# Who copies the first three tiles of the third branch's projection out of PSUM: VectorE instead of ScalarE

## The chip, the cores and the metric

One NeuronCore of one Trainium2 chip runs the whole program. The metric is the device time of one execution in microseconds (us), as the median of several runs.

## The reference, cut to what matters

One decoder layer on 512 tokens of width 1024, in float32. Four mixers run beside each other on one projection of the normalised input, each is projected back to 1024 channels, weighted by a sigmoid gate, and summed:

```python
z = h @ w_in                       # columns: aq ak av iq ik iw pin gu gv sq sk sv, then four gates
o_a = sparse_indexed_attention(...)   # 4 heads of 64, each query keeps its top 128 keys
o_b = multiscale_pool(...)
o_c = chunked_spatial_gating(...)
o_d = stick_breaking_attention(...)
o = jnp.stack([o_a, o_b, o_c, o_d], axis=2)
proj = jnp.einsum('bsnw,nwd->bsnd', o, w_branch)         # 256 -> 1024 for each branch
merged = jnp.sum(sigmoid(gl) * proj, axis=2)
x = x + merged @ w_out
x = x + swiglu_ffn(rms_norm(x), ...)
```

The sparse attention of a block of 128 queries is: logits for 4 heads, plus a bias that masks the keys not chosen, a row maximum, exp, division by the row sum, and the product with the values.

## The kernel before, in words

**Weights in chunks.** All weights come in chunks of 1 MB, numbered c. SyncE loads chunk c into one of two raw buffers (L395) once VectorE has finished the low half of chunk c-2. Each chunk is split into two reduced-precision parts: ScalarE writes the high part `w_hi` (L541, or in two halves at L549), then VectorE subtracts and writes the low part `w_lo` (L977). TensorE multiplies with three matmuls for each product (`three`, L1539: lines 1541, 1542, 1543) and can start a chunk only when both parts are there (semaphores `hi_ready`, `lo_ready`, L1846 and L1847).

**Order of the chunks around the change.** Chunk 15 is the projection of the first branch (m=0), 16 that of m=1, 17 to 20 are the gates of m=1, 21 is the projection of the third branch (m=2), 22 to 25 are its gates, 26 is the projection of m=3 and 27 to 30 are its gates. `PROJ_AT` is [15, 16, 21, 26]. "Chunk 21" below is the projection that the change touches.

**A projection chunk** (`proj_chunk`, L1572) makes 8 tiles d=0 to 7, each of 128 output channels by 512 tokens, from 6 matmuls. Tile f goes to PSUM bank f%2, so TensorE has two banks to fill in turn and waits in `take_bank` (L1545) until the tile two before has been copied out (semaphores `taken0`, `taken1`). For chunks 16, 21 and 26 ScalarE copies each tile to `branch` in SBUF (`branch_tiles`, L618, copy at L630). Into these copies it puts the two halves of the high part of the next chunk's weights: before tile 1 and before tile 4. VectorE does the low part of that chunk when the second half is there. For chunk 15 VectorE itself empties the banks (L1331), multiplying with the gates on the way.

**Gates.** For chunks 17 to 20 and 22 to 25 ScalarE writes the sigmoid of each tile from PSUM to `two` (L685), VectorE multiplies it with the tile of `branch` (`gated`, L1279), and GpSimd adds the result to `merged` (L521).

**The sparse attention lies between the chunks**, one block b of queries at a time, by `slot(c)` on each engine, which runs behind the engine's own work on chunk c. `A_SLOT` is 16. Block 2 goes: in slot 20 TensorE computes the values of block 1 (L1773) and the logits of block 2 (L1755, L1757), then goes on with chunk 21. VectorE adds the bias and takes the maxima (`biased`, L1198), ScalarE then negates them and takes the exponentials (`soft_max`, L748 and L750), and VectorE takes the reciprocal of the sums and multiplies (`normalised`, L1205 and L1207). In slot 21, behind chunk 21, TensorE transposes the result (L1764) and ScalarE copies it out (L759).

**Order on each engine.** Every engine works its instructions in the order of the code and stops at a wait. ScalarE's order here is: sigmoids of chunk 20, `soft_max(2)`, `branch_tiles(21)` with the halves of chunk 22, `turned_prob(2)`, the high part of chunk 23, sigmoids of chunk 22. VectorE's is: low part of chunk 21, products of chunk 20, `biased(2)`, `normalised(2)`, low part of chunk 22, five rounds of the search for the largest 8 scores of block 3 (`top_rounds(21)`, L1081 and L1082), low part of chunk 23, products of chunk 22, `biased(3)`.

Of the kernel before, what the change touches and what calls it, by code (L numbers as in the profile page):

```python
# [42 lines left out]
def hybrid_layer(nc, x, mix_norm, w_in, attn_q_norm, attn_k_norm, pool_w, pool_scale, gmlp_norm,  # L43
# [4 lines left out]
    TT = SEQ // P  # L48
    KT = D // P
# [18 lines left out]
    chunks = []  # L68
# [28 lines left out]
    PROJ_AT = [c for c in range(MIXER_CHUNKS) if chunks[c][0] == "proj"]  # L97
# [23 lines left out]
    fill_at, f = [], 0  # L121
# [10 lines left out]
    def w_at(c):  # L132
        if c < MIXER_CHUNKS:
            return c % 2 * CHUNK
        if chunks[c][0] == "ffn":
            return (7 * QUAD, 0)[(c - MIXER_CHUNKS) % 2]
        at = PLAIN[0] if c in PLAIN else max(d for d in down_at if d <= c)
        return (8 * QUAD, 0)[(c - at) % 2]
# [4 lines left out]
    def before_at(c):  # L143

        a, z = w_at(c), w_at(c) + w_size(c)
        return max((d for d in range(c) if w_at(d) < z and a < w_at(d) + w_size(d)), default=None)

    with ExitStack() as ctx:
        top = [(nc.sbuf_base + 63) // 64 * 64]

        def place(name, shape, dt=F32, at=None):
            size = 4
            for n in shape[1:]:
                size *= n
            if at is None:
                at = top[0]
                top[0] += (size + 63) // 64 * 64
            return nc.alloc_sbuf_tensor_at(name, shape, dt, offset=at)

        def sem(name):  # L160
            return ctx.enter_context(nc.semaphore(name))
# [23 lines left out]
        branch = place("branch", [P, KT, SEQ], at=L0)  # L185
# [107 lines left out]
        bank = [ctx.enter_context(nc.psum_tensor(f"bank{i}", [P, 512], F32)) for i in range(8)]  # L293
# [40 lines left out]
        S = {n: sem(n) for n in names}  # L334
        taken = [S["taken0"], S["taken1"]]
        raw_ready = [S["raw0"], S["raw1"]]
        x_ready = [S["x0"], S["x1s"], S["x2"], S["x3"]]
        hi_ready, lo_ready, filled = S["hi_ready"], S["lo_ready"], S["filled"]
# [15 lines left out]
        def head_rows(h):  # L354

            return (slice(0, 64), slice(64, 128))[::1 if h % 2 == 0 else -1]
        D_SLOT, A_SLOT = 10, 16
        IDX_SLOT = 2

        def split_early(c):  # L360

            return IDX_SLOT <= c - 2 < IDX_SLOT + 4

        def wait_taken(eng, f):

            eng.wait_ge(taken[f % 2], f // 2 + 1)
# [5 lines left out]
        def wait_used(eng, c):  # L372

            kind, _, _, _, what = chunks[c]
            if kind == "ffn":
                eng.wait_ge(S["product_done"], 7 * (wino_index[c] + 1))
            elif kind != "acc":
                eng.wait_ge(filled, fill_at[c + 1])
            elif what[3]:
                eng.wait_ge(S["acc_filled"], TT * (what[0] + 1))  # L380
            else:
                eng.wait_ge(S["acc_chunks"], sum(k[0] == "acc" and not k[4][3] for k in chunks[:c + 1]))
# [143 lines left out]
        def _(act):  # L526
# [16 lines left out]
            def split_half(c, second):  # L543
                n = chunks[c][2] * chunks[c][3] // 2
                part = slice(n * second, n * (second + 1))
                if not second:
                    act.wait_ge(raw_ready[c % 2], 16 * (c // 2 + 1))
                    wait_used(act, before_at(c))
                ins = nact.activation(w_hi[:, w_at(c) + part.start:w_at(c) + part.stop], raw[:, c % 2, part], ACT.Copy)  # L549
                if second:  # L550
                    ins.then_inc(hi_ready, 1)
# [66 lines left out]
            def branch_tiles(c):  # L618

                m = chunks[c][4]  # L620
                for d in range(KT):
                    if d in (1, 4):
                        split_half(c + 1, d == 4)
                    f = fill_at[c] + d
                    if m == 1:
                        wait_taken(act, fill_at[c - 1] + d)
                    else:
                        act.wait_ge(S["gated"], (m - 2) * KT + d + 1)
                    act.wait_ge(filled, f + 1)
                    nact.activation(branch[:, d, :], bank[f % 2][:, :], ACT.Copy).then_inc(taken[f % 2], 1)  # L630
# [61 lines left out]
            def indexer(b):  # L692

                for h in range(IDX_HEADS):
                    n = IDX_HEADS * (b - 1) + h
                    act.wait_ge(S["idx_filled"], n + 1)
                    if n >= 4:
                        act.wait_ge(S["relu_used"], n - 3)
                    w = P * (b + 1)
                    nact.activation(relu[:, n % 4, 0:w], bank[2 + n % 4][:, 0:w], ACT.Relu).then_inc(S["relu_ready"], 1)  # L700
# [68 lines left out]
            def slot(c):  # L769
                if IDX_SLOT <= c < IDX_SLOT + 3:  # L770
                    indexer(c - IDX_SLOT + 1)
                if c == 1:
# [190 lines left out]
        def _(dve):  # L963
            vec = nc.vector
            steps = [0]

            def link(ins):
                steps[0] += 1
                ins.then_inc(S["dve_step"], 1)
                dve.wait_ge(S["dve_step"], steps[0])  # L970
# [9 lines left out]
            def split_half(c, second):  # L980
                n = chunks[c][2] * chunks[c][3] // 2
                part = slice(n * second, n * (second + 1))
                at = slice(w_at(c) + part.start, w_at(c) + part.stop)
                dve.wait_ge(hi_ready, c + 1)
                ins = vec.tensor_tensor(w_lo[:, at], raw[:, c % 2, part], w_hi[:, at].bitcast(F32), ALU.subtract)
                ins.then_inc(lo_ready if second else S["dve_step"], 1)
                steps[0] += not second
# [199 lines left out]
            def biased(b):  # L1187
# [8 lines left out]
                for h in range(HEADS):  # L1196
# [2 lines left out]
                                             scalar=TAKEN, op0=ALU.add, op1=ALU.max,  # L1199
                                             accum_out=top_logit[:, h:h + 1]).then_inc(S["biased_ready"], 1)  # L1200

            def normalised(b):
                w = P * (b + 1)
                dve.wait_ge(S["prob_summed"], HEADS * (b + 1))
                link(vec.reciprocal(inv_total[:, :], total[:, :]))  # L1205
                for h in range(HEADS):
                    vec.tensor_scalar(prob[:, h, 0:w], prob[:, h, 0:w], inv_total[:, h:h + 1], None, ALU.mult)\  # L1207
                        .then_inc(S["prob_ready"], 1)
# [7 lines left out]
            def top_rounds(c):  # L1216
                for b, n in rounds.get(c, ()):
                    take_top(b, n, last=(c == max(d for d in rounds for e, _ in rounds[d] if e == b)))

            def slot(c):  # L1220
                if c == 1:
                    constants()
                if IDX_SLOT <= c < IDX_SLOT + 3:
                    if c == IDX_SLOT:
                        dve.wait_ge(S["iw_ready"], 1)
                        dve.wait_ge(S["const_made"], 4)
                    indexer(c - IDX_SLOT + 1)
                if c == 4:
                    wait_chunk_taken(dve, 3)
                    norm_sums()  # L1230
                if c == 5:
                    norm_scale()
                if c == 7:
                    gate_mixed()
                if c == 9:
                    out_parts(1, 6, PSC)
                if D_SLOT <= c < D_SLOT + HEADS + 2:
                    k = c - D_SLOT
                    if k >= 2:
                        stick_total(k - 2)  # L1240
                    if 1 <= k <= HEADS:
                        weights_low(k - 1)
                    if k < HEADS:
                        left(k)
                    if 2 <= k < HEADS:
                        stick_out(k - 2)
                    if k == HEADS + 1:
                        stick_out(HEADS - 2)
                        stick_out(HEADS - 1)
                        dve.wait_ge(S["q_hi_ready"], MT + 1)  # L1250
                        stack_low(True, qT, lambda x: slice(x, HEADS, 2), lambda own, x: q_lo[own, x:HEADS:2, :], 1.0)
                        dve.wait_ge(S["k_hi_ready"], MT + 1)
                        stack_low(False, kT, lambda x: slice(x, HEADS, 2), None, 1.0).then_inc(S["stacks_ready"], 1)
                if A_SLOT <= c <= A_SLOT + 2 * TT:
                    b, odd = (c - A_SLOT) // 2, (c - A_SLOT) % 2
                    if not odd and b < TT:
                        biased(b)
                        top_rounds(c)
                        normalised(b)
                    elif not odd:  # L1260
                        out_parts(3, 6, None)
# [23 lines left out]
            for c in range(MIXER_CHUNKS):  # L1285
# [37 lines left out]
                if (kind, what) == ("proj", 0):  # L1323
                    for d in range(KT):
                        if d in (2, 5):
                            split_half(c + 1, d == 5)
                        f = fill_at[c] + d
# [680 lines left out]
```

## Time and profile before

| | us |
|---|---|
| median of 3 runs | 799.18 (798.92 to 799.45) |
| the profiled execution, its own time | 797.43 |
| its span in the trace | 795.7 |
| TensorE busy in the span | 785.4 |
| VectorE busy | 516.8 |
| ScalarE busy | 369.6 |
| GpSimd busy | 89.4 |

Times in the trace are microseconds from the start of the span. PE is TensorE's matmul, PEld its weight load, which overlaps the matmuls, DVE is VectorE, ACT is ScalarE, POOL is GpSimd, SP is SyncE. Matmuls overlap in the records: one of 512 columns has a duration of 0.39 us, while the next one starts 0.23 us after it. A busy time of 99% is therefore no statement on how well the engine is used; gaps between starts are.

### The profile page before, as it was taken

The page shows a single profiled execution, that of the slowest core. Times are in us where ns is not written, and L with a number is a line of the kernel's source. Part 1 is how long each engine was busy: PE and PEld are TensorE (multiplying, and loading weights), DVE is VectorE, ACT ScalarE, POOL GpSimd, SP SyncE. Part 2 cuts the span into 40 slices and gives each one's busy share as a digit, 9 for nine tenths or more (in the row PEclk, how much of TensorE's full clock was granted, in tenths as well). Part 3 has the DMA queues.
Part 4 walks back from the last instruction along what each step waited for, and adds up shares of the span by engine and source line. Part 5 has one row for each costly group of instructions (what it writes and reads, how often), then busy time and mean ns, then how long its engine had stood idle before and what let it go on. Part 6 is the DMA issues. An engine that isn't in the chain of part 4 may idle for free.

```text
span 795.7 us, 11821 instructions
## 1 busy us (share of the span) xinstructions
PE 785.4 (99%) x4801; PEld 698.1 (88%) x4801; DVE 516.8 (65%) x765; ACT 369.6 (46%) x562; POOL 89.4 (11%) x97
## 2 busy tenths in 40 slices
PE   8999999999999989999999999999999999999997
PEld 8999888888888868888888899999988899999886
DVE  5536987889788855323435799888513588886331
ACT  7635444455664374442424566555411255554220
POOL 7100040335003301212300000000000000000000
PEclk9999999999999999999999999999999999999999
DMA  9363122311313311524234033333333323333321
GB/s 272 101 181 101 59 66 93 101 59 54 106 53 106 106 54 53 212 70 142 78 112 155 1 106 107 106 107 107 106 106 106 106 76 102 105 106 98 125 80 53
DMA packets 63830, 80.39 MB, mean 101 GB/s; under 512 B 1876, under 2 KB 52128, under 8 KB 63776
## 3 DMA queue, kind: packets, MB, share of 16 engines
q1 hardware_dynamic: 63024, 78.65, 31.2%
q0 software_dynamic: 752, 0.99, 0.5%
q8 instruction: 38, 0.62, 0.3%
q14 instruction: 16, 0.13, 0.1%
HBM read 75.96 MB, written 2.10 MB: 98 GB/s over the span
## 4 chain that ended last, share of the span: by engine, by line
PE 96%; ACT 1%; DVE 1%; DMA 1%; issue 0%; ACTq 0%; DVEq 0%
PE bank L1541 22%; PE bank L1543 22%; PE bank L1542 22%; PE bank L1942 8%; PE bank L1944 8%; PE bank L1943 8%; PE bank L1773 1%; PE bank L1743 1%; PE bank L1764 1%; PE bank L1677 1%; DMA raw<-in_w_in_dram 0%; DMA x_sb<-in_x_dram 0%; PE bank L1732 0%; PE bank L1867 0%; PE bank L1717 0%; DVE x_sb L1500 0%
## 5 line engine op out<-in xcount | busy, mean ns | idle before, releaser
L977 DVE TENSOR_TENSOR w_lo<-raw,w_hi 128x2048 fp32r<-128x2048 f32 (+1 forms) x46 | 106.2, 2310 | 107.8 <-ACT w_hi L541 98.3
L1541 PE MATMUL bank<-h_hi,w_hi 128*128 128x512 f32 (+1 forms) x416 | 155.5, 374 | 0.6 <-DVE h_lo L1349 0.5
L1543 PE MATMUL bank<-h_hi,w_lo 128*128 128x512 f32 (+1 forms) x416 | 153.6, 369 | 0.0
L1542 PE MATMUL bank<-h_lo,w_hi 128*128 128x512 f32 (+1 forms) x416 | 153.4, 369 | 0.0
L541 ACT ACTIVATE w_hi<-raw 128x2048 fp32r<-128x2048 f32 (+1 forms) x45 | 83.7, 1861 | 81.7 <-PE bank L1543 81.5
L1541 PEld LDWEIGHTS bank<-h_hi,w_hi 128*128 128x128 f32 x416 | 78.4, 188 | 14.0 <-DVE h_lo L1349 0.7
L1543 PEld LDWEIGHTS bank<-h_hi,w_lo 128*128 128x128 f32 x416 | 78.4, 188 | 13.3
L1942 PE MATMUL bank<-t_hi,w_hi 128*128 128x256 f32 x320 | 89.7, 280 | 0.0
L1542 PEld LDWEIGHTS bank<-h_lo,w_hi 128*128 128x128 f32 x416 | 78.4, 189 | 12.8
L1944 PE MATMUL bank<-t_hi,w_lo 128*128 128x256 f32 x320 | 89.3, 279 | 0.0
L1943 PE MATMUL bank<-t_lo,w_hi 128*128 128x256 f32 x320 | 89.3, 279 | 0.0
L1541 PE MATMUL bank<-w_hi,a_hi 128*128 128x512 f32 x176 | 68.5, 389 | 0.0
L1542 PE MATMUL bank<-w_lo,a_hi 128*128 128x512 f32 x176 | 68.5, 389 | 0.0
L1543 PE MATMUL bank<-w_hi,a_lo 128*128 128x512 f32 x176 | 68.5, 389 | 0.0
L1944 PE MATMUL bank<-h_hi,w_lo 128*128 128x256 f32 x240 | 68.1, 284 | 0.0
L1942 PE MATMUL bank<-h_hi,w_hi 128*128 128x256 f32 x240 | 68.0, 283 | 0.0
L1943 PE MATMUL bank<-h_lo,w_hi 128*128 128x256 f32 x240 | 67.9, 283 | 0.0
L1942 PEld LDWEIGHTS bank<-t_hi,w_hi 128*128 128x128 f32 x320 | 60.2, 188 | 0.0
L1944 PEld LDWEIGHTS bank<-t_hi,w_lo 128*128 128x128 f32 x320 | 60.1, 188 | 0.0
L1943 PEld LDWEIGHTS bank<-t_lo,w_hi 128*128 128x128 f32 x320 | 60.1, 188 | 0.0
L521 POOL TENSOR_TENSOR merged<-merged,two 128x512 f32<-128x512 f32 x24 | 38.4, 1601 | 167.9 <-DVE two L1279 167.9
L685 ACT ACTIVATE two<-bank 128x512 f32<-128x512 f32 x24 | 14.3, 598 | 73.0 <-PE bank L1543 66.5
(243 smaller groups left out, 1600.9 us busy)
## 6 DMA issues: line engine op xcount, KB each, us to landing
raw<-in_w_in_dram SPq DMA_DIRECT2D x26, 1024.0 KB, 5.4
raw<-in_w_ffn_gate_dram SPq DMA_DIRECT2D x11, 1024.0 KB, 5.3
raw<-in_w_ffn_up_dram SPq DMA_DIRECT2D x11, 1024.0 KB, 5.3
raw<-in_w_ffn_down_dram SPq DMA_DIRECT2D x10, 1024.0 KB, 5.0
raw<-in_w_branch_dram SPq DMA_DIRECT2D x4, 1024.0 KB, 4.9
raw<-in_w_out_dram SPq DMA_DIRECT2D x4, 1024.0 KB, 5.0
x_sb<-in_x_dram SPq DMA_DIRECT2D x4, 512.0 KB, 6.0
x_sb<-in_x_dram SPq DMA_DIRECT2D x1, 2048.0 KB, 11.3
```

What stands on the lines that cost most here:

```text
L521: pool.tensor_tensor(merged[:, d, :], merged[:, d, :], two[:, y % 2, :], ALU.add)\
L541: nact.activation(w_hi[:, w_at(c):w_at(c) + n], raw[:, c % 2, 0:n], ACT.Copy).then_inc(hi_ready, 1)
L685: ins = nact.activation(two[:, y % 2, :], wide, ACT.Sigmoid)
L977: vec.tensor_tensor(w_lo[:, at], raw[:, c % 2, 0:n], w_hi[:, at].bitcast(F32), ALU.subtract)\
L1541: mm(dst, l_hi, r_hi, start=start, stop=False)
L1542: mm(dst, l_hi, r_lo, start=False, stop=False)
L1543: return mm(dst, l_lo, r_hi, start=False, stop=stop)
L1677: mm(bank[2 + n % 4][:, 0:w], iq_stack[0:96, h, b * P:(b + 1) * P], ik_stack[0:96, 0:w], start=True, stop=True).then_inc(S["idx_filled"], 1)
L1743: last = mm(bank[4 + 3 * (h % 2)][:, j * P:SEQ], sv2[:, j, h, :], part[:, SB_COL[j]:SB_COL[j] + w], start=(part is weight_hi and j == 0), ...
L1942: mm(dst, l_hi, r_hi, start=begin and k == 0, stop=False, skip_group_check=True)
L1943: mm(dst, l_hi, r_lo, start=False, stop=False, skip_group_check=True)
L1944: ins = mm(dst, l_lo, r_hi, start=False, stop=k == KT // 2 - 1, skip_group_check=True)
```

## The change

VectorE copies tiles 0, 1 and 2 of chunk 21 into `branch`, behind `biased(2)` and ahead of `normalised(2)`. ScalarE's loop over that chunk begins with tile 3, and puts the two halves of chunk 22 before tiles 4 and 6. The other two projections that ScalarE copies (chunks 16 and 26) stay as they were.

```diff
+        SHARED_PROJ, SHARED_TILES = PROJ_AT[2], 3
+        assert (SHARED_PROJ - 1 - A_SLOT) % 2 == 0 and SHARED_PROJ - 1 < A_SLOT + 2 * TT
@@ ScalarE
             def branch_tiles(c):
                 m = chunks[c][4]
-                for d in range(KT):
-                    if d in (1, 4):
-                        split_half(c + 1, d == 4)
+                halves_at = (SHARED_TILES + 1, SHARED_TILES + 3) if c == SHARED_PROJ else (1, 4)
+                for d in range(SHARED_TILES if c == SHARED_PROJ else 0, KT):
+                    if d in halves_at:
+                        split_half(c + 1, d == halves_at[1])
                     f = fill_at[c] + d
@@ VectorE
+            def shared_tiles(c):
+                for d in range(SHARED_TILES):
+                    f = fill_at[c] + d
+                    dve.wait_ge(S["gated"], (chunks[c][4] - 2) * KT + d + 1)
+                    dve.wait_ge(filled, f + 1)
+                    vec.tensor_copy(branch[:, d, :], bank[f % 2][:, :]).then_inc(taken[f % 2], 1)
@@ VectorE, slot(c)
                         biased(b)
                         top_rounds(c)
+                        if c == SHARED_PROJ - 1:
+                            shared_tiles(SHARED_PROJ)
                         normalised(b)
```

## Rows read from the trace of the kernel before

**Rows 1.** The page: the chain that ended last, share of the span by engine.

```profile
PE 96%; ACT 1%; DVE 1%; DMA 1%; issue 0%; ACTq 0%; DVEq 0%
```

**Rows 2.** Waits of TensorE: who waited for whom, total us, times, longest.

```profile
PE bank L1541 <- ACT branch L630: 3.0, 1, 3.0
```

**Rows 3.** Stretches: from:to, length, busy PE, PEld, DVE, ACT, POOL, PEclk, DMA.

```profile
281.00:284.30 3.30, 0.31 (x2) 0.00 (x0) 0.46 (x2) 3.29 (x11) 0.00 (x0) 1.00 0.01 2
```

**Rows 4.** Timeline of TensorE, chunk 21 and behind it: start, us, line, [idle before].

```profile
278.41 0.39 PE L1541 MATMUL bank<-o_hi,w_hi 128*128 128x512 f32 x1
...
279.79 0.39 PE L1541 MATMUL bank<-o_hi,w_hi 128*128 128x512 f32 x1
...
280.92 0.39 PE L1543 MATMUL bank<-o_hi,w_lo 128*128 128x512 f32 x1
284.30 0.50 PE L1541 MATMUL bank<-o_hi,w_hi 128*128 128x512 f32 x1 [3.00 <-ACT branch L630]
...
287.21 0.39 PE L1541 MATMUL bank<-o_hi,w_hi 128*128 128x512 f32 x1
...
292.66 1.47 PE L1764 MATMUL bank<-ident,prob 128*128 128x128 f32 x12
293.88 0.47 PE L1541 MATMUL bank<-h_hi,w_hi 128*128 128x512 f32 x1
```

**Rows 5.** Timeline of ScalarE in the same stretch.

```profile
283.68 0.57 ACT L630 ACTIVATE branch<-bank 128x512 f32<-128x512 f32 x1
...
287.47 0.60 ACT L630 ACTIVATE branch<-bank 128x512 f32<-128x512 f32 x1 [0.82 <-PE bank L1543]
287.97 1.05 ACT L549 ACTIVATE w_hi<-raw 128x1024 fp32r<-128x1024 f32 x1
```

**Rows 6.** Timeline of VectorE in the same stretch.

```profile
279.63 0.08 DVE L1198 DVE_READ_ACCUMULATOR2_ANT top_logit<- 128x1 f32 x1
283.80 0.18 DVE L1205 RECIPROCAL inv_total<-total 128x4 f32<-128x4 f32 x1 [4.08 <-ACT prob L750]
284.02 1.41 DVE L1207 TENSOR_SCALAR prob<-prob,inv_total 128x384 f32<-128x384 f32 x4
289.05 2.29 DVE L977 TENSOR_TENSOR w_lo<-raw,w_hi 128x2048 fp32r<-128x2048 f32 x1 [3.62 <-ACT w_hi L549]
291.26 0.69 DVE L1081 MAX8 best<-score 128x8 f32<-128x512 f32 x1
...
299.18 2.29 DVE L977 TENSOR_TENSOR w_lo<-raw,w_hi 128x2048 fp32r<-128x2048 f32 x1
...
307.61 0.69 DVE L1198 CUSTOM_DVE_ANT_0 prob<-bank,score 128x512 f32<-128x512 f32 x1 [1.15 <-PE bank L1757]
```

**Rows 7.** Line 1331 (durations min/median/max): VectorE empties the banks of chunk 15.

```profile
L1331 DVE TENSOR_TENSOR merged<-bank,gates x8: 681/688/693, 206.4 to 215.7; 128x512 f32<-128x512 f32 x8
```

**Rows 8.** Timelines of TensorE, VectorE and the weight load within chunk 15.

```profile
210.01 0.40 PE L1541 MATMUL bank<-o_hi,w_hi 128*128 128x512 f32 x1
...
210.21 0.69 DVE L1331 TENSOR_TENSOR merged<-bank,gates 128x512 f32<-128x512 f32 x1 [0.45 <-PE bank L1543]
...
213.32 0.68 DVE L1331 TENSOR_TENSOR merged<-bank,gates 128x512 f32<-128x512 f32 x1
...
214.06 0.19 PEld L1541 LDWEIGHTS bank<-o_hi,w_hi 128*128 128x128 f32 x1 [0.22 <-DVE merged L1331]
```

**Rows 9.** Timelines of VectorE and GpSimd at the start of chunk 20.

```profile
269.45 3.38 DVE L977 TENSOR_TENSOR w_lo<-raw,w_hi 128x2048 fp32r<-128x2048 f32 x1
272.75 1.77 DVE L1279 TENSOR_TENSOR two<-two,branch 128x512 f32<-128x512 f32 x1
...
269.01 4.96 POOL L521 TENSOR_TENSOR merged<-merged,two 128x512 f32<-128x512 f32 x2 [14.78 <-DVE two L1279]
```

**Rows 10.** Timeline of GpSimd: the first addition behind chunk 21.

```profile
302.15 1.29 POOL L521 TENSOR_TENSOR merged<-merged,two 128x512 f32<-128x512 f32 x1 [23.50 <-DVE two L1279]
```

**Rows 11.** DMA issues: KB each, us from issue to landing.

```profile
raw<-in_w_in_dram SPq DMA_DIRECT2D x26, 1024.0 KB, 5.4
```

## The prediction

> **What bounds the kernel now.** I read the page first: 96% of the chain that ended last is TensorE's own work [rows 1]. So a gain has to come out of a gap in TensorE's stream, and other engines' work counts only where it makes such a gap. The waits of TensorE are the second view: one of them, 3.0 us, is far longer than the others, and it is for ScalarE's copy of a projection tile [rows 2]. The table of stretches shows what each engine did meanwhile: from 281.00 to 284.30 ScalarE was busy for 3.29 us, VectorE for 0.46, GpSimd not at all, and the granted clock of TensorE was full, 1.00 [rows 3]. The timelines then give the places. TensorE starts tile 0 of chunk 21 at 278.41, tile 1 at 279.79 and the last matmul of tile 1 at 280.92; then both banks are full, and tile 2 starts at 284.30 [rows 4]. ScalarE, which would empty them, is in the exponentials of block 2 up to 283.68 [rows 5]. VectorE finished the maxima at 279.71 and waits for these same exponentials until 283.80 [rows 6]. An idle engine stands beside a busy one, and the tiles wait for the busy one.
>
> **What goes.** Without a wait the matmuls follow each other by 0.227 us: tile 1 begins at 279.79 and would end its six starts at 280.92 + 0.23 = 281.15, which is 1.36 us for a tile [rows 4]. Tile 2 would start at 281.15, not 284.30: 3.15 us. Tiles 2 and 3 took 287.21 - 284.30 = 2.91 us where two tiles want 2.72, a slow first matmul and a second short wait for ScalarE [rows 4]: 0.19 us more. In sum 3.34 us, and the transposes behind the chunk would begin at 289.32 and not at 292.66.
>
> **What VectorE adds.** Three copies of 128x512 from PSUM. No such copy stands in the trace. From below, it can't cost less than nothing. From above, the nearest row is VectorE's product of a PSUM bank with a tile of SBUF, same shape, 0.69 us [rows 7]; I take that, since the bank is the same and a copy has one operand less. A farther upper end is a VectorE instruction of this width at its slowest, 1.77 us, in which GpSimd was also at work [rows 9]; here GpSimd starts its next addition only at 302.15, after 23.5 us of idling [rows 10]. In chunk 15 VectorE starts on a tile 0.20 us after TensorE starts the next tile (210.21 against 210.01), and the weight load of the waiting tile starts 0.06 us behind VectorE's end (213.32 + 0.68 against 214.06) [rows 8]. So: tile 0 is copied from 279.99 to 280.68, tile 1 from 281.35 to 282.04, tile 2 from 282.71 to 283.40. Tile 2 wants its bank by about 280.9, if the weight load goes one matmul (0.23 us) ahead of 281.15, tile 3 by 282.3, tile 4 by 283.6: each bank is free 0.2 us before that. VectorE is ready for tile 0, since the maxima end at 279.71 [rows 6]. Behind these copies on VectorE stands `normalised(2)`, whose exponentials come at 283.80 in any case: the copies end 0.4 us before, so it isn't moved, and it ends at 285.43 [rows 6], long before the transposes at 289.32 that want it. The 2.1 us of copies are hidden in a wait of 4.08 us [rows 6]; without that cover they would stand on the way to the low part of chunk 22.
>
> The Trainium skill has a sentence that speaks against the choice of engine ("ScalarE: Activation LUTs", the part on the pipeline's stages): ScalarE is placed closer to PSUM, VectorE closer to SBUF. The rows agree in sign, 0.60 us on ScalarE against 0.69 on VectorE [rows 5, 7]; by the rule the copies stay on ScalarE and the wait stays, by the rows the 0.09 us for each tile lies inside a period of 1.36.
>
> **What ScalarE loses and what moves.** Three copies go from its stream. It is free at 283.68, as before. A tile's copy starts 0.26 us after TensorE starts the next tile (287.47 against 287.21) [rows 4, 5]. Tile 4 starts at 281.15 + 2 x 1.36 = 283.87, so tile 3 is copied at 284.13; then the first half of chunk 22's high part, 1.05 us, to about 285.7; tile 4 just after, to 286.2, and tile 6 wants that bank at 286.4. Tile 5 is copied at 286.85, and the second half starts 0.50 us later, as it does now (287.97 against 287.47) [rows 5]: 287.35 to 288.40. The load of chunk 22 is not moved: it is released by the low part of chunk 20, issued long before, and takes 5.4 us [rows 11].
>
> **What is late next.** The low part of chunk 22. VectorE starts it 0.03 us behind the second half and needs 2.29 us [rows 5, 6]: 288.43 to 290.72, and the first matmul of chunk 22 can start 0.1 us later, at 290.81. TensorE wants it after its transposes, which take 293.88 - 292.66 = 1.22 us [rows 4]: at 289.32 + 1.22 = 290.54. So a new wait of 0.27 us, with a slow first matmul some 0.3 to 0.4. Before, that low part was ready at 291.34 for a start at 293.88: the halves come 0.6 us sooner, the tiles 3.3 us. The range of this term is 0 (the hand-over as quick as it can be) to 1.4: the same subtraction took 3.38 us beside GpSimd's additions [rows 9] where it takes 2.29 here, 1.09 more.
>
> **Behind it.** VectorE's search starts at 290.7 in place of 291.26, so the low part of chunk 23 comes 0.6 us sooner than 299.18 + 2.29, at 300.9 [rows 6]. TensorE wants it after the two tiles of chunk 22, block 2's values and block 3's logits; the maxima of block 3 show the last of these, 307.61 - 293.88 = 13.7 us behind the start of chunk 22 [rows 4, 6], so at 304.6 at the earliest: covered by 3.7 us. VectorE's maxima of block 3 waited 1.15 us for TensorE's logits [rows 6] and go forward with them. Loads of chunks 24 and 25 are released by these two low parts, 0.6 us sooner each, and take 5.4 us [rows 11]. From there on every engine is released by TensorE's tiles, directly or by a chain, so I carry the shift to the end unchanged.
>
> **Sum.** 3.34 - 0.34 = 3.0 us. The profiled execution has 797.43 us, its span 795.7: they would be 794.4 and 792.7. The median of the runs is 1.75 us above the profiled execution; the shift is the same there, 799.18 - 3.0 = 796.2 us. A measurement of this kernel can tell about 0.2%, 1.6 us, from no change.
>
> **The rivals.**
> First, the forecast: 795.8 (no new wait) to 796.7. For it speaks that each step is tied to rows within 30 us of the place, the VectorE reads of full banks excepted.
> Second, the limit moves to the low part of chunk 22 more than I reckon: a split of 3.38 us, or a second half that ScalarE does one tile later. Then 1.1 to 1.4 us more is given back, and the time is 797.4. Against it: GpSimd, beside which the long one lies, is idle here [rows 9, 10].
> Third, the time is given back, or the change doesn't do what it says: another release that isn't tied to TensorE (a load, VectorE's search) comes in time for today's schedule alone, or VectorE's copies start only when the exponentials have ended. The price is up to the whole 3.3 us: 798 to 799.5. Against it: the one release that I found not to move with TensorE, VectorE's search with the low part of chunk 23 behind it, is covered by 3.7 us; and `biased(2)` ends at 279.71, before tile 0 is full.
> Fourth, on the other side: VectorE empties a bank slowly. The three copies are in series, and tile 4 can't start before the third has ended, at 279.99 + 3c for a copy of c us. Tile 4 starts at 283.87 without a wait; the gain of 3.0 is used up when it starts at 286.9, that is at c = 2.3. At c = 3.38, the longest VectorE row that I read [rows 9], the third ends at 290.1, 6.3 us late, and the time is 799.2 + 3.3 = 802.5. Against it: all eight VectorE reads of a full bank in chunk 15 took 0.68 to 0.69 us [rows 7]. At 1.77 us, tile 4 starts 1.5 us late and the time is 797.7, no gain that counts but no loss.
>
> **How the numbers follow.** Forecast 0.78, second 0.10, third 0.09, fourth 0.03. Faster than 797.6 are the forecast and the second, 0.88; same is the third, 0.09; slower the fourth, 0.03. The predicted time is the forecast's, 796.2. The range takes in the forecast's own ends, 795.8 to 796.7, the second's 797.4 and, below, as much as the three runs of before spread, 0.5 us: 795.3 to 797.4.
>
> **What would show it.** In the profile after: no wait of TensorE for ScalarE's copies; three VectorE copies of about 0.69 us at 280.0, 281.35 and 282.7; the reciprocal still at 283.8; the transposes at 289.3; a short wait of chunk 22 for VectorE's low part at 290.5 to 290.9; a span near 792.7. The prediction is wrong if tile 2 starts later than 281.5, if chunk 22 starts later than 291.5, or if a later mark, such as the maxima of block 3, stands less than 2.5 us before its place now, 307.61.

## The result, and the profile after

| | before | changed |
|---|---|---|
| median, us | 799.3 (797.55 to 799.46, 6 runs) | 793.57 (793.34 to 794.19, 6 runs) |
| profiled execution | 797.43 | 793.36 |
| its span | 795.7 | 791.6 |

The ratio is 0.9928, interval 0.9918 to 0.9938: 5.7 us faster, where 3.0 was forecast and 795.3 was the lower end. Between the two profiled executions lie 4.1 us.

At the place of the change the profile is as forecast. TensorE's waits in the changed kernel, the view of [rows 2], have no line with ScalarE's copy any more:

```profile
PE bank L1626 <- POOL ident L450: 1.6, 1, 1.6
PE bank L1641 <- DVE h_lo L1023: 0.7, 2, 0.4
PE bank L1556 <- DVE h_lo L1364: 0.5, 1, 0.5
PE bank L1556 <- DVE merged L1346: 0.2, 1, 0.2
```

Its timeline, which answers to [rows 4] (all TensorE lines are 15 higher), begins chunk 21 at 278.45 and goes through tile 2 without a gap; the transposes start at 289.35, chunk 22 at 290.86:

```profile
278.45 0.39 PE L1556 MATMUL bank<-o_hi,w_hi 128*128 128x512 f32 x1
...
281.18 0.39 PE L1556 MATMUL bank<-o_hi,w_hi 128*128 128x512 f32 x1
...
289.35 1.47 PE L1779 MATMUL bank<-ident,prob 128*128 128x128 f32 x12
290.86 0.47 PE L1556 MATMUL bank<-h_hi,w_hi 128*128 128x512 f32 x1
```

VectorE's timeline answers to [rows 6]. The three copies take 0.69 us each, the reciprocal is not moved, the low part of chunk 22 begins at 288.46, and the maxima of block 3 stand at 304.60 where they stood at 307.61. Below them, from PEld, the first weight load of chunk 22 with its new wait:

```profile
280.09 0.69 DVE L1213 COPY branch<-bank 128x512 f32<-128x512 f32 x1 [0.34 <-PE bank L1558]
281.45 0.69 DVE L1213 COPY branch<-bank 128x512 f32<-128x512 f32 x1 [0.67 <-PE bank L1558]
282.81 0.69 DVE L1213 COPY branch<-bank 128x512 f32<-128x512 f32 x1 [0.67 <-PE bank L1558]
283.85 0.18 DVE L1218 RECIPROCAL inv_total<-total 128x4 f32<-128x4 f32 x1 [0.34 <-ACT prob L755]
...
288.46 2.29 DVE L982 TENSOR_TENSOR w_lo<-raw,w_hi 128x2048 fp32r<-128x2048 f32 x1 [2.99 <-ACT w_hi L553]
...
304.60 0.69 DVE L1203 CUSTOM_DVE_ANT_0 prob<-bank,score 128x512 f32<-128x512 f32 x1 [1.15 <-PE bank L1772]
...
290.82 0.19 PEld L1556 LDWEIGHTS bank<-h_hi,w_hi 128*128 128x128 f32 x1 [0.25 <-issue]
```

ScalarE's timeline, for [rows 5]: its first copy is tile 3, and the second half starts at 287.38.

```profile
284.16 0.60 ACT L635 ACTIVATE branch<-bank 128x512 f32<-128x512 f32 x1 [0.35 <-PE bank L1558]
...
287.38 1.05 ACT L553 ACTIVATE w_hi<-raw 128x1024 fp32r<-128x1024 f32 x1
```

From chunk 22 to its last matmul TensorE is 3.0 us earlier: 293.88 became 290.86, the maxima of block 3 moved by as much, and the last matmul went from 791.04 to 788.03. The other 1.1 us of the 4.1 lie behind that matmul. The last matmul and SyncE's wait for the last stores, before:

```profile
791.04 0.39 PE L1543 MATMUL bank<-w_hi,a_lo 128*128 128x512 f32 x1
...
SPq L148 <- DMA out_dram<-x_sb: 2.8, 1, 2.8
```

and in the changed kernel:

```profile
788.03 0.39 PE L1558 MATMUL bank<-w_hi,a_lo 128*128 128x512 f32 x1
...
SPq L148 <- DMA out_dram<-x_sb: 1.7, 1, 1.7
```

The span ends 4.7 us behind the last matmul before, 3.6 us behind it after. So two things were open: this end, and why the medians are 5.7 us apart where the traced executions are 4.1 apart.

### The profile page after: what moved, and what is told of

It reads as the page before. It is cut to its first block, busy times and chain, and to the rows that moved or that the text cites. A ratio compares the mean times of both kernels' runs of the same rounds, so it can differ in the third digit from the quotient of the medians.

```text
span 791.6 us, 11821 instructions
## 1 busy us (share of the span) xinstructions
PE 785.3 (99%) x4801; PEld 698.3 (88%) x4801; DVE 519.0 (66%) x768; ACT 368.2 (47%) x559; POOL 89.5 (11%) x97
## 4 chain that ended last, share of the span: by engine, by line
PE 98%; DVE 1%; ACT 0%; issue 0%; POOL 0%; POOLq 0%
PE bank L1556 22%; PE bank L1558 22%; PE bank L1557 22%; PE bank L1957 8%; PE bank L1959 8%; PE bank L1958 8%; PE bank L1626 1%; PE bank L1788 1%; PE bank L1758 1%; PE bank L1779 1%; PE bank L1692 1%; PE bank L1747 0%; PE bank L1770 0%; PE bank L1882 0%; PE bank L1732 0%; PE bank L1772 0%
```

## The experiments

**Two more traces of the kernel before.** No edit. The traced execution of before had been one of the short ones.

> The kernel before, unchanged, run again. Its runs so far are of two lengths: 797.43 and 797.55 us in two executions, 798.92 to 799.46 in five; the trace shown is of a 797.43 us one. Theory A (the wait at chunk 21 itself is longer in the long executions, because ScalarE's table load or exponentials, which end it, take longer there): a trace of a long execution shows tile 2 of chunk 21 starting 1.5 to 2 us later than 284.30, and the rest of TensorE's stream moved by that much. Theory B (the extra time lies elsewhere: start, end, or another wait): tile 2 starts at 284.3 as before and the extra 1.5 to 2 us stand at another place.

> The same kernel a second time, for a second trace. Same expectations as the first; whichever of the two shows a span near 797.5 us decides between A and B.

The first run came to 799.59 us (span 797.8), the second to 799.5 (797.7); ten runs of it went from 797.48 to 800.63. Its wait at chunk 21 is unchanged, 3.0 us. The place in theory A is right and its mechanism is wrong: ScalarE is not late. Tile 2 starts 0.54 us later than 284.30, and a shift of this size is there from the first chunks on (tile 0 of chunk 21 stands at 278.95, not 278.41). What differs is the speed of the matmuls behind the wait (the first new trace):

```profile
284.84 0.50 PE L1541 MATMUL bank<-o_hi,w_hi 128*128 128x512 f32 x1 [2.99 <-ACT branch L630]
...
285.87 0.63 PE L1542 MATMUL bank<-o_lo,w_hi 128*128 128x512 f32 x1
286.29 0.63 PE L1543 MATMUL bank<-o_hi,w_lo 128*128 128x512 f32 x1
...
288.85 0.59 PE L1543 MATMUL bank<-o_hi,w_lo 128*128 128x512 f32 x1
289.28 0.41 PE L1541 MATMUL bank<-o_hi,w_hi 128*128 128x512 f32 x1
```

Eight steps from 285.87 to 289.28 take 0.43 us each and not 0.23: 3.41 us in place of 1.81, 1.6 us lost. The table of stretches shows the granted clock (the last three columns are PEclk, DMA share and GB/s); first in this trace, then in the first trace of before:

```profile
286.00:290.00 4.00, 4.00 (x13) 3.12 (x12) 0.00 (x0) 1.27 (x3) 0.00 (x0) 0.59 0.00 0
```

```profile
286.00:290.00 4.00, 4.00 (x19) 3.28 (x19) 0.95 (x1) 2.63 (x4) 0.00 (x0) 1.00 0.00 0
```

13 matmuls against 19 in the same 4 us, at a granted clock of 0.59 in the mean: part of the stretch ran at 1.2 GHz and the rest at 2.4. What the engine did before it fell was to stand for 3.0 us [rows 2] and then to start four more matmuls, 0.23 to 0.34 us apart; behind eight slow ones, it was back at the full rate. The second new trace has the same wait and the same loss, with the first step of 0.43 us at 286.41 where this one has it at 285.87. The Trainium skill, "TensorE: Matmul & The Clock Gate", Part 1, states that a TensorE that idles is gated down to 1.2 GHz, and of the rise at a kernel's start that its place varies from run to run. The traces agree with the first (0.43 us from start to start, behind the wait), and the fall varies in a like way here: it is missing in one trace of this kernel and begins at two different places in the two others.

**The halves alone.**

```diff
-                for d in range(KT):
-                    if d in (1, 4):
-                        split_half(c + 1, d == 4)
+                halves_at = (4, 6) if c == PROJ_AT[2] else (1, 4)
+                for d in range(KT):
+                    if d in halves_at:
+                        split_half(c + 1, d == halves_at[1])
```

> Only the second part of the change: ScalarE copies all eight tiles of chunk 21 as before, but the halves of chunk 22 stand before tiles 4 and 6 and not before 1 and 4. My account of the change: the wait for the exponentials stays (tile 2 at 284.2 to 284.4), the second half ends about 1.4 us later than at 289.02, the low part of chunk 22 is ready at about 292.7 and wanted at 293.8, so there is no new wait: the time is that of before within 0.3 us. Rival (the place of the halves alone brings part of the 5.7 us): at least 1 us faster than before.

799.32 us against 799.04 on the same chip, ratio 1.0005 (0.9992 to 1.0018): the halves don't bring the 1 us that the rival asked for. The new wait that I had excluded here is there, though, 0.24 us ahead of the first weight load of chunk 22:

```profile
296.46 0.19 PEld L1542 LDWEIGHTS bank<-h_hi,w_hi 128*128 128x128 f32 x1 [0.24 <-issue]
```

The second half moves with the tiles, so it stands as close before chunk 22 with the wait at tile 2 as without it; my expectation had put it too early.

**Two tiles, one tile.** The changed kernel with `SHARED_TILES` of 2 and of 1, the halves kept at 4 and 6.

> VectorE copies two tiles and not three; halves at 4 and 6. My account: tile 2 starts at 281.2 as in the changed kernel, but tile 4 needs the bank that ScalarE empties only behind the exponentials (283.7 to 284.3), so tile 4 starts at 284.3 and not at 283.9, and chunk 22 starts about 0.5 us later than 290.86. Slower than the changed kernel by 0.3 to 0.6 us if all executions are like the traced ones. If theory A holds (ScalarE is late by up to 2 us in many executions), this kernel, which still waits for ScalarE, keeps part of that: slower than the changed kernel by 1.5 to 2.5 us in the median.

> VectorE copies tile 0 only, halves at 4 and 6. TensorE goes on to tile 2 at 281.2 and stands before tile 3, at 282.5, until ScalarE has emptied tile 1's bank, 284.3: an idle stretch of 1.8 us and not 3.0. Linear theory (only the stretch costs): chunk 22 starts 1.8 to 2.0 us later than in the changed kernel, time about 795.4. Clock theory says the same if so short a stretch never lowers the clock (runs within 1 us of each other), and up to 1.6 us more, with scatter, if it does.

| tiles by VectorE | longest wait at chunk 21 | start of tile 0 of chunk 21 to start of chunk 22 | median, us (range) |
|---|---|---|---|
| 0 (before) | 3.0 | 15.47 | 799.04 (chip of the run with two), 799.51 (chip of the run with one) |
| 1 | 1.6 | 14.35 | 796.32 (796.08 to 796.62) |
| 2 | 0.3 | 12.99 | 794.26 (793.71 to 794.43) |
| 3 (changed) | none | 12.41 | 793.57 (793.34 to 794.19) |

TensorE's wait in the runs with one and with two tiles:

```profile
PE bank L1556 <- ACT branch L635: 1.6, 1, 1.6
```

```profile
PE bank L1556 <- ACT branch L635: 0.3, 1, 0.3
```

All nine of these runs have a granted clock of 0.999 or 1.000 over the whole run, and they don't scatter: 0.5 us (one tile) and 0.7 us (two) from the fastest to the slowest, against 4.4 and 3.3 for before on the same chips. With a wait of 1.6 us no run shows the lower clock; only the wait of 3.0 us has scatter with it. At the place, two tiles cost 0.6 us more than three (12.99 against 12.41), the upper end of the 0.3 to 0.6 that I expected; the medians are 0.7 apart, but from different chips. One tile costs 1.9 us at the place (14.35), as expected, but the time is 0.9 us above my 795.4: its trace runs 0.4 us late from the first chunks on, and its span ends 4.3 us behind the last matmul, not 3.6.

**A longer wait.** In the kernel before, ScalarE copies tile 0 of chunk 21 three times:

```diff
                     act.wait_ge(filled, f + 1)
+                    if (c, d) == (PROJ_AT[2], 0):
+                        for _ in range(2):
+                            link(nact.activation(branch[:, d, :], bank[f % 2][:, :], ACT.Copy))
```

> The kernel before with a wait made longer: ScalarE copies tile 0 of chunk 21 three times, so tile 2 starts some 1.2 us later, at 285.5. If only the wait costs, the time is 1.2 us above before, with before's scatter. If the fall of the clock depends on how long TensorE stands, the lower clock appears in every execution or for longer: 2 to 3.5 us above before in the median.

TensorE waits 4.3 us; 801.01 us against 799.51, 1.5 us more by the medians and 1.8 by the ratio, 1.0023 (1.0010 to 1.0036). All ten runs have a mean clock of 0.998 or less, none the 0.999 to 1.000 of the short runs of before. That bears the clock theory in that the fall now comes every time. In the trace it isn't a longer one: again 1.6 us are lost, from 286.76 on. The median price is little more than the added 1.3 us, because most runs of before had the fall too; the 2 to 3.5 us that I gave it were too much.

**TensorE works while it waits.** In the kernel before, ten matmuls into a bank that nobody uses, ahead of tile 2 (they add work and change no result):

```diff
                 for d in range(KT):
+                    if c == PROJ_AT[2] and d == 2:
+                        pe.wait_ge(S["biased_ready"], HEADS * 3)
+                        for _ in range(10):
+                            mm(bank[2][:, :], w_hi[:, w_at(c):w_at(c) + P], o_hi[:, O_SET[m], 0, :], start=True, stop=True)
                     b = take_bank(fill_at[c] + d)
```

> The kernel before, with ten matmuls of 512 columns into a bank that nobody uses, put ahead of tile 2 of chunk 21: the wait for ScalarE stays where it is, and TensorE works in it (10 x 0.227 = 2.3 us of the 3.3). Clock theory (behind the idle stretch TensorE's clock falls to 1.2 GHz in most executions, and eight matmuls then take 0.43 us from start to start and not 0.23): tile 2 starts at the same place, about 284.3, no matmul behind it is 0.43 us apart, and the runs lie together at 797.4 to 798.3, where those of before scatter from 797.4 to 800.7; median 1 to 1.5 us below before. Rival (the scatter of before has another cause): scatter and median as before.

Tile 2 starts 3.4 us after tile 1's last matmul started (284.91 against 281.53), as before, and nothing behind it is slow:

```profile
281.75 2.43 PE L1578 MATMUL bank<-o_hi,w_hi 128*128 128x512 f32 x10
284.91 0.50 PE L1541 MATMUL bank<-o_hi,w_hi 128*128 128x512 f32 x1 [0.73 <-ACT branch L630]
...
285.48 0.39 PE L1543 MATMUL bank<-o_hi,w_lo 128*128 128x512 f32 x1
```

```profile
284.80:290.00 5.20, 5.09 (x22) 4.10 (x23) 1.57 (x5) 4.00 (x7) 0.00 (x0) 1.00 0.00 0
```

The median is 797.8 us (797.27 to 798.66) against 799.51 (797.43 to 801.85), ratio 0.9979 (0.9969 to 0.9988). Idle or busy, TensorE needs the same time at this place: from tile 0 of chunk 21 to chunk 22 it takes 15.48 us here and 15.47 in the trace of before. What goes with the useless matmuls is 1.7 us of lower clock, a little more than the 1 to 1.5 that I expected, and all ten runs have a mean clock of 0.999 or 1.000. They lie where the eight runs of before at that clock lie on this chip, 798.0 us. The rival is out.

**A few more steps on VectorE.** For the end of the span. In the kernel before, where the change puts its copies, three copies of four columns that nobody reads:

```diff
                         top_rounds(c)
+                        if c == PROJ_AT[2] - 1:
+                            for i in range(3):
+                                dve.wait_ge(S["gated"], i + 1)
+                                dve.wait_ge(S["biased_ready"], i + 1)
+                                vec.tensor_copy(newton[:, 4 * i:4 * i + 4], best[:, 0:4])
                         normalised(b)
```

> The kernel before with three tiny VectorE copies (128x4, each with two waits that are long met) put between the maxima and the normalisation, where the change puts its copies: nothing of the tiles changes. Between TensorE's last matmul and the end of the span lie 4.6 to 4.8 us in all traces of the kernel before and its variants, and 3.6 us where VectorE has copies more; in the first a fetch of instructions falls into the last stores, at 792.2, in the second it falls before them. Fetch theory (the fetch is VectorE's, its place is fixed by the count of its instructions): here it falls before the stores, the end of the span comes 3.5 to 3.7 us behind the last matmul, and the median is 1.0 us below before. Rival (the shorter end has to do with the tiles or with the clock): 4.6 to 4.8 us, and the time of before.

The last matmul and SyncE's wait for the last stores in this run, whose span is 796.7:

```profile
793.10 0.39 PE L1548 MATMUL bank<-w_hi,a_lo 128*128 128x512 f32 x1
...
SPq L148 <- DMA out_dram<-x_sb: 1.7, 1, 1.7
```

3.6 us, as in the changed kernel, while the wait at chunk 21 is still 3.0 and the matmuls behind it are still at 1.2 GHz in this trace (0.43 us apart from 285.54 on). The DMA view of single microseconds shows what moved. In the trace of before, 792 to 793, in the middle of the last stores, the packet of an instruction fetch stands among 193 of theirs and takes 6.3% of 16 engines' microsecond, 1.0 us on one engine:

```profile
q1 hardware_dynamic: 193, 0.36, 99.2%
q14 instruction: 1, 0.01, 6.3%
```

With more steps on VectorE the same packet comes at 779 to 780, alone, and takes 0.5 us:

```profile
q14 instruction: 1, 0.01, 3.2%
```

That is 13.6 us ahead of the start of the last matmul (779.5 against 793.10); in the trace of before the fetch starts 1.3 us behind it (792.4). In the changed kernel it comes at 774.4 to 775.0, again 13.6 us ahead, with two tiles at 787.9 to 788.4, 0.5 us ahead, and both have the short end. With one tile it starts at 791.1, 0.8 us behind the last matmul, takes 0.3 us, and the end is 4.3 us. With ten matmuls more on TensorE it stays 1.3 us behind (793.0, end 4.5 us), and with two copies more on ScalarE as well (795.4, end 4.7 us). So it is what was added to VectorE's instructions that moves it. The median is 798.65 against 799.51, ratio 0.999 (0.998 to 1.0001): the sign and size fit 1.0 us, but under this kernel's scatter the times alone don't settle it; the ends of the traces do.

**Both small additions, and the changed kernel beside them.** The kernel before with the ten matmuls and the three small copies, and the changed kernel on the same chip.

> The kernel before with both small additions: the ten matmuls in TensorE's wait and the three tiny copies on VectorE. If the clock's fall (1.7 us between the medians of the run with the matmuls and of before) and the fetch in the last stores (1.1 us at the end of the trace) are the two terms that my prediction lacked and if they add up, this kernel is 2.6 to 2.9 us faster than before in the median, has neither the scatter nor the long end (3.6 us behind the last matmul), and stands 3.0 us above the changed kernel, which is the term that I had. Rival (one of the two contains the other, or the changed kernel gains by something else): less than 2 us faster than before, or more than 3.6 us above the changed kernel.

> The changed kernel on the same chip as the two others: 5.5 to 6 us faster than before, all runs within 1 us, no wait at chunk 21, end of the span 3.6 us behind the last matmul.

On this chip before has 798.61 us (797.41 to 800.59), the kernel with the matmuls and the steps 796.72 (796.0 to 797.36), the changed one 793.71 (793.21 to 793.86). Between the last two lie 3.0 us, as expected, and both have the short end (3.6 us). The distances to before are below what I had expected, 1.9 us (ratio 0.9978, 0.9968 to 0.9987) for 2.6 to 2.9, and 4.9 (0.9943, 0.9930 to 0.9955) for 5.5 to 6. The 1.9 lies just inside the less than 2 us that I had set for the rival; its other mark, more than 3.6 us above the changed kernel, isn't met. Before itself is 0.9 us faster here than on the chip of the last experiments. The lower clock came less often (nine of 15 runs by their mean clock, against 22 of 30), and the runs with it stand at 798.65 us against 799.5 there, only 1.1 us above those without it on this chip. So the 3.0 us of the wait is confirmed, and so is that the two other terms are there; their sizes, 1.6 and 1.1 in the traces, come out smaller here, 1.1 for the clock and 0.8 for the end (797.5 against 796.72), and why is open.

**Halves one tile sooner**, for a version that is faster still: in the changed kernel

```diff
-                halves_at = (SHARED_TILES + 1, SHARED_TILES + 3) if c == SHARED_PROJ else (1, 4)
+                halves_at = (SHARED_TILES, SHARED_TILES + 2) if c == SHARED_PROJ else (1, 4)
```

> The changed kernel with the halves of chunk 22 before tiles 3 and 5, one tile sooner. The low part of chunk 22 is then ready at about 289.4, before the transposes end at 290.6, so the last short wait (0.25 us of the weight load, 0.3 with the slow matmul) goes; against that tile 3's copy ends at 285.3 and tile 5's bank is wanted at 285.0, a new wait of 0.1 to 0.2 us. Chunk 22 starts 0.0 to 0.2 us sooner than 290.86; time that of the changed kernel within 0.3 us. If a wait at tile 5 is longer than the one removed: up to 0.3 us slower.

793.68 us against 793.71, no difference, though two of the five runs lie at 792.6 and 792.7. Chunk 22 starts 0.1 us sooner at the place. Its weight load no longer waits, but tile 5's does, for a little longer than the 0.1 to 0.2 us that I expected:

```profile
285.70 0.19 PEld L1556 LDWEIGHTS bank<-o_hi,w_hi 128*128 128x128 f32 x1 [0.29 <-ACT branch L635]
```

## Why the prediction was right and wrong

**What goes** was right: 3.34 us, the transposes at 289.32 in the text and 289.35 in the trace (which is 0.04 us late from the start of the chunk).

**What VectorE adds** was right: 0.69 us for a copy, taken from the nearest row; the copies start 0.1 us later than I put them, inside the 0.2 us of slack, and the normalisation isn't moved (283.80, 283.85). VectorE's 0.69 us against ScalarE's 0.60 is now a copy against a copy, where the prediction had set a product against one; the 0.09 us a tile stay hidden, as it had them.

**What is late next** was right: the low part of chunk 22 from 288.46 (288.43 in the text), chunk 22 at 290.86 (290.81 to 290.9), a new wait of 0.25 us. The profile puts it down to "issue"; that VectorE's subtraction is what TensorE waits for follows from its end, 290.75, and from the run with the halves one tile sooner, in which it is gone.

**Behind it** was right for TensorE: the shift of 3.0 us is there at the last matmul unchanged. It was wrong for the end. "I carry the shift to the end unchanged" took the last stores as fixed, and they were 1.1 us shorter, because VectorE's longer program moved an instruction fetch out of them.

**The sum** failed at the step to the median: "The median of the runs is 1.75 us above the profiled execution; the shift is the same there". That distance was not a constant around the kernel. The traced execution of before was one in which the clock didn't fall; in most it does, behind the very wait that the change removes. Of the 64 runs of before that were timed beside the edited kernels, on three chips, 20 had a mean clock of 0.999 or 1.000 and a median of 797.7 us, 44 had less and a median of 799.5. That is 1.8 us over all chips and 1.5, 1.5 and 1.1 us within each one. The traced fall cost 1.6 us, the experiment with the matmuls 1.7.

So two terms that I had set to nothing failed: what the change does to the distance from the trace to the median, and what it does to the stretch behind the last matmul. Measured, the first is 1.66 us (799.30 - 797.43 = 1.87 before, 793.57 - 793.36 = 0.21 after) and the second 1.06 us. With the 3.01 us at the last matmul, which I had, they are the 5.73 us between the medians. That the traced fall, 1.6 us, gives the first of the two so closely is in part luck: the size differs between chips, and the first chunks alone put a trace up to 0.6 us later or 0.2 us earlier than the first one.

**The rivals.** I priced slower copies, a later split and a lost gain, and no case with a gain above 3.4 us. In the rows that I read, PEclk was 1.00 in the wait [rows 3] in that one execution; a median 1.75 us above it, with three runs within 0.5 us of each other, was the sign that it was not the typical one. The Trainium skill's rule above was a rival by itself, on the faster side, and I left it out.

**Open.** Eight of the 64 runs of before have a mean clock of 0.996 and a median of 800.6 us, 1.4 us above the other 36 with a lower clock. No trace shows one, so whether the lower clock lasts longer there or comes a second time isn't known; and three runs at 0.998 are as long, 800.4 to 800.6. Why 3.0 us of idling has the fall in most executions and not in all isn't shown either. That the fetch delays the stores by sharing a DMA engine with them is argued: it takes 1.0 us there against 0.5 alone, and in the run with the halves alone, where it took 1.2 us, the end is the longest of all, 4.8 us; but with one tile it took only 0.3 and the end is still 4.3. Shown is that moving it out of the stores shortens the end.

## What to carry to other kernels

A wait of TensorE can cost more than its length: at 1.6 us no run showed a lower clock, at 3.0 us some of the matmuls behind it ran at half speed in most executions, at 4.3 us in all ten, and a single trace can be one of the few without it. Where a median lies a microsecond or two above the traced execution, take the difference apart before carrying it over, and look at the mean clock of each run. To tell clock from wait, fill the wait with matmuls that nobody uses. And an idle engine beside a busy one that holds the banks can take some of its copies, as many as end before its own next release.

## What the runs showed of the hardware that I had not expected

- Behind 3.0 us of idling, eight matmuls of 512 columns at 0.43 us from start to start where 0.23 is usual, 1.6 us in all, beginning after TensorE resumed and not with it (285.87 against 284.84; 0.7 to 1.6 us behind it over the traces that show it), in 44 of 64 runs by their mean clock. Behind 4.3 us of idling the trace shows the same 1.6 us, and all ten runs have the lower clock. With 2.4 us of matmuls in the same stretch: in none of ten.
- An instruction fetch of one packet, 0.5 us when alone, took 0.9 to 1.2 us among the last stores, and those traces end 4.5 to 4.8 us behind the last matmul, against 3.6 us where it falls earlier. Three more copies on VectorE with their waits, 500 us before, moved it from 1.3 us behind the last matmul to 13.6 us ahead of it.
